# Root mean squares of a two-block transformer: tokens on the partitions of a few columns, then laid out as rows by a product with the identity

## The reference, cut to what matters

```python
def rms_norm(x, g):
    xf = x.astype(jnp.float32)
    y = xf * lax.rsqrt(jnp.mean(xf * xf, axis=-1, keepdims=True) + EPS)
    return (y * g.astype(jnp.float32)).astype(x.dtype)

h = rms_norm(x, norm1_g[l]) * (1.0 + sc1) + sh1      # first block, layers 0 and 1
```

```python
y = rms_norm(y.reshape(bsz, seq, SSM_GROUPS, D_INNER // SSM_GROUPS), ssm_norm_g[l].reshape(SSM_GROUPS, D_INNER // SSM_GROUPS))
```

## Time and profile before

| | us |
|---|---|
| median of 3 runs | 2081.39 (2077.65 to 2081.71) |
| time of the profiled execution | 2083.6 |
| span in the profile | 2081.5 |
| PE busy | 1824.0 (88%) |
| PEld busy | 1730.1 (83%) |
| POOL busy | 1173.7 (56%) |
| DVE busy | 1144.6 (55%) |
| ACT busy | 879.1 (42%) |
| mean granted clock of TensorE | 0.900 |

### The profile page before, as it was taken

How to read it: one execution, slowest core, us unless ns; L and a number is a source line. 1 busy time by engine, 2 the same in 40 slices (tenths; PEclk the granted TensorE clock), 3 DMA queues, 4 the chain that set the end, 5 groups by cost and what they waited for, 6 DMA issues and landing times.

```text
span 2081.5 us, 34069 instructions
## 1 busy us (share of the span) xinstructions
PE 1824.0 (88%) x13514; PEld 1730.1 (83%) x13514; DVE 1144.6 (55%) x1840; ACT 879.1 (42%) x1427; POOL 1173.7 (56%) x480
## 2 busy tenths in 40 slices
PE   8987689999868999679498999967999897967999
PEld 8977689888667999679497888857999796767999
DVE  3289657656633886459946657553685227343410
ACT  2233454544334664224264544333565443334542
POOL 1256665354345899437484445525788676025886
PEclk8689899999979999769799999989999998569999
DMA  6233355343323558334355543524465644013554
GB/s 244 81 111 126 128 173 203 132 162 136 124 91 118 191 189 283 118 102 141 103 168 187 193 132 109 175 80 134 142 185 182 224 154 125 1 40 122 184 186 137
DMA packets 85949, 302.76 MB, mean 145 GB/s; under 512 B 9888, under 2 KB 12960, under 8 KB 85536
## 3 DMA queue, kind: packets, MB, share of 16 engines
q1 hardware_dynamic: 85792, 300.59, 43.8%
HBM read 299.50 MB, written 1.05 MB: 144 GB/s over the span
## 4 chain that ended last, share of the span: by engine, by line
PE 70%; DVE 16%; issue 4%; DVEq 4%; ACT 2%; POOL 2%; DMA 1%; SPq 0%; ACTq 0%; POOLq 0%
PE gemm_bank L1292 53%; PE turn_bank L1400 2%; PE score_bank L1292 2%; POOL w_lo L365 2%; PE outp_bank L1520 1%; PE outp_bank L1385 1%; PE score_bank L1418 1%; PE turn_bank L1367 1%; DVE work L770 1%; DVE work L754 1%; PE score_bank L1367 1%; DVEq L753 1%; PE score_bank L1417 1%; DMA ada_w<-in_w_ada 1%; DVE qkv L781 1%
## 5 line engine op out<-in xcount | busy, mean ns | idle before, releaser
L365 POOL TENSOR_TENSOR w_lo<-w_raw,w_hi 128x1024 fp32r<-128x1024 f32 (+1 forms) x476 | 1173.5, 2473 | 896.2 <-ACT w_hi L383 891.3
L383 ACT ACTIVATE w_hi<-w_raw 128x1024 fp32r<-128x1024 f32 (+1 forms) x476 | 492.6, 1038 | 727.2 <-PE gemm_bank L1292 699.6
L1292 PE MATMUL gemm_bank<-h_hi,w_hi 128*128 128x256 f32 x1984 | 577.7, 291 | 95.4 <-DVE conv L681 32.1
L1292 PE MATMUL gemm_bank<-h_lo,w_hi 128*128 128x256 f32 x1984 | 569.5, 287 | 0.0
L1292 PE MATMUL gemm_bank<-h_hi,w_lo 128*128 128x256 f32 x1984 | 569.2, 287 | 0.0
L1292 PEld LDWEIGHTS gemm_bank<-h_hi,w_hi 128*128 128x128 f32 x1984 | 388.3, 196 | 108.4 <-DVE h_lo L681 33.0
L1292 PEld LDWEIGHTS gemm_bank<-h_lo,w_hi 128*128 128x128 f32 x1984 | 388.2, 196 | 0.1
L1292 PEld LDWEIGHTS gemm_bank<-h_hi,w_lo 128*128 128x128 f32 x1984 | 387.4, 195 | 0.0
L1292 PE MATMUL gemm_bank<-w_hi,h_hi 128*128 128x256 f32 (+3 forms) x736 | 216.9, 295 | 21.5 <-DVE h_lo L681 9.6
L1292 PE MATMUL gemm_bank<-w_lo,h_hi 128*128 128x256 f32 (+3 forms) x736 | 215.8, 293 | 0.0
L1292 PE MATMUL gemm_bank<-w_hi,h_lo 128*128 128x256 f32 (+3 forms) x736 | 215.5, 293 | 0.0
(11 more groups left out here) (256 smaller groups left out, 2814.8 us busy)
## 6 DMA issues: line engine op xcount, KB each, us to landing
w_raw<-in_stream SPq DMA_DIRECT2D x458, 512.0 KB, 3.5
ada_w<-in_w_ada SPq DMA_DIRECT2D x80, 512.0 KB, 4.6
ada_first<-in_w_ada SPq DMA_DIRECT2D x16, 512.0 KB, 11.3
w_raw<-in_stream SPq DMA_DIRECT2D x8, 256.0 KB, 2.6
alibi_sb<-in_alibi SPq DMA_DIRECT2D x1, 1920.0 KB, 8.4
rows_sb<-in_rows SPq DMA_DIRECT2D x1, 1536.0 KB, 11.6
residual<-in_x_t SPq DMA_DIRECT2D x1, 1024.0 KB, 7.2
out_x<-residual SPq DMA_DIRECT2D x4, 256.0 KB, 4.5
```

The costliest lines, as they stand in the source:

```text
L365: nc.gpsimd.tensor_tensor(w_lo[:, s, 0:n], w_raw[:, s, 0:n], w_hi[:, s, 0:n].bitcast(f32), ALU.subtract).then_inc(lo_ready, 1)
L383: A(w_hi[:, s, 0:n], w_raw[:, s, 0:n], ACT.Copy).then_inc(hi_ready, 1)
L1292: ins = M(o, a, b, start=first and i == 0, stop=last and i == len(passes) - 1, skip_group_check=True)
```

## The change

The sum of squares of a token no longer comes as a row repeated on all partitions. The tile of squares becomes the stationary operand, 128 features x 128 tokens, and one column of ones the moving one; the result is one column, with a token on each partition. The 256 tokens give two columns. `square_sum_x` issues 16 such products for 8 before (`column_sum`), and `square_sum` 2 for one. DVE, ACT and again DVE work on 2 columns (an x norm) or 4 (a y norm) in the new tile `rcol`; `root_columns` has the same five operations as `rsqrt`. Then PE lays them out as a row on all partitions: the stationary operand is a column broadcast over 128 columns, the moving one the identity (`row_of_columns`, two products of 128 columns for each row of 256 tokens). The row stays in the PSUM bank, and the scalar_tensor_tensor operations read it from there. The bank is given free behind these, no longer behind the first read of it.

Where the rows are formed: in an x norm right behind the sum (`root_row_x`); for the first norm behind the first of the 8 shift columns; for the first half's y norm in the second half behind chunks 16 to 19 and ahead of the transposes; for the second half's behind chunks 30 and 31. The wait of PE for the constants' arrival stands ahead of the shift columns now.

```diff
             def sum_root(l, which):
-                A(rs[:, 0, :], rs[:, 1, :], ACT.Sqrt).then_inc(x_root, 1)
+                act.wait_ge(x_mean, 2 * l + which + 1)
+                A(rcol[:, 0:TT], rcol[:, 4:4 + TT], ACT.Sqrt).then_inc(x_root, 1)
...
-                    for gi in range(2):
-                        b, k = T.use(l, ts + gi)
-                        act.wait_ge(T.read[b], k + 1)
-                        A(rs[:, gi, :], work[:, gi, 0:SEQ], ACT.Sqrt).then_inc(y_root, 1)
+                    act.wait_ge(y_mean, 2 * l + hf + 1)
+                    A(rcol[:, 0:4], rcol[:, 4:8], ACT.Sqrt).then_inc(y_root, 1)
...
+            def root_columns(n):
+                r, v, w = rcol[:, 0:n], rcol[:, 4:4 + n], rcol[:, 8:8 + n]
+                V.reciprocal(r, r)
+                dve.drain()
+                V.tensor_tensor(w, r, r, ALU.mult)
+                dve.drain()
+                V.tensor_tensor(w, w, v, ALU.mult)
+                dve.drain()
+                V.tensor_scalar(w, w, -0.5, 1.5, ALU.mult, ALU.add)
+                dve.drain()
+                V.tensor_tensor(r, r, w, ALU.mult)
+                return dve.drain()
...
-                dve.wait_ge(o_full, 6 * l + (6 if which else 1))
+                dve.wait_ge(x_sum, n + 1)
+                V.tensor_scalar(rcol[:, 4:4 + TT], O.bank[b][:, 2 * SEQ - TT:2 * SEQ], 1.0 / D, EPS, ALU.mult, ALU.add
+                                ).then_inc(x_mean, 1)
                 if l < DEPTH and which:
                     mods(ada_column(6 * l + 3), KT, O.bank[b][:, SEQ:SEQ + KT])
-                V.tensor_scalar(rs[:, 1, :], O.bank[b][:, 0:SEQ], 1.0 / D, EPS, ALU.mult, ALU.add).then_inc(O.read[b], 1)
                 dve.wait_ge(x_root, n + 1)
-                dve.drain()
-                rsqrt(rs[:, 0, :], rs[:, 1, :], work[:, 0, 0:SEQ])
+                root_columns(TT).then_inc(x_col, 1)
+                dve.wait_ge(o_full, 6 * l + (6 if which else 1))
                 for kt in range(KT):
-                    stt(sq[:, kt, :], XT[:, kt, :], gain[:, kt:kt + 1], rs[:, 0, :], ALU.mult, ALU.mult).then_inc(h_scaled, 1)
+                    stt(sq[:, kt, :], XT[:, kt, :], gain[:, kt:kt + 1], O.bank[b][:, 0:SEQ], ALU.mult, ALU.mult).then_inc(h_scaled, 1)
+                dve.drain().then_inc(O.read[b], 1)
...
-                    dve.wait_ge(y_root, 4 * l + 2 * hf + 2)
-                    dve.drain()
-                    rsqrt(rs[:, 0:2, :], work[:, 0:2, 0:SEQ], work[:, 2:4, 0:SEQ])
+                    ins.then_inc(y_mean, 1)
+                    dve.wait_ge(y_root, 2 * l + hf + 1)
+                    root_columns(4).then_inc(y_col, 1)
                     for f in range(8):
                         t = 8 * hf + f
-                        stt(zg[:, t, :], zg[:, t, :], col("ssmn", t), rs[:, f // 4, :], ALU.mult, ALU.mult).then_inc(y_scaled, 1)
+                        b, k = T.use(l, ts + f // 4)
+                        if f % 4 == 0:
+                            dve.wait_ge(y_row, 4 * l + 2 * hf + f // 4 + 1)
+                        stt(zg[:, t, :], zg[:, t, :], col("ssmn", t), T.bank[b][:, 0:SEQ], ALU.mult, ALU.mult).then_inc(y_scaled, 1)
+                        if f % 4 == 3:
+                            dve.drain().then_inc(T.read[b], 1)
...
-                    ins = M(out[:, 0:SEQ], ones[:, 0:P], sq[:, kt, :], start=kt == 0, stop=kt == KT - 1)
-                ins.then_inc(o_full, 1)
+                    for tt in range(TT):
+                        ins = column_sum(out, tt, sq[:, kt, tt * P:(tt + 1) * P], kt == 0, kt == KT - 1)
+                ins.then_inc(x_sum, 1)
+
+            def column_sum(out, tt, squares, first, last):
+                c = 2 * SEQ - TT + tt
+                return M(out[:, c:c + 1], squares, ones[:, 0:1], start=first and tt == 0, stop=last, skip_group_check=True)
+
+            def row_of_columns(out, c):
+                for tt in range(TT):
+                    ins = M(out[:, tt * P:(tt + 1) * P], rcol[:, c + tt:c + tt + 1].to_broadcast([P, P]), ident[:],
+                            start=True, stop=True)
+                return ins
+
+            def root_row_x(l, which):
+                i = (O_N2 if which else O_N1) if l < DEPTH else (O2_N2 if which else O2_N1)
+                b, k = O.use(l, i)
+                pe.wait_ge(x_col, 2 * l + which + 1)
+                row_of_columns(O.bank[b], 0).then_inc(o_full, 1)
...
             def norm_sum(l, which):
                 square_sum_x(l, which)
+                root_row_x(l, which)
                 return half_h(l, which)
...
+            pe.wait_ge(set_up, 1)
             for a in range(KT):
                 ada_first_column(a)
-            pe.wait_ge(set_up, 1)
+                if a == 0:
+                    root_row_x(0, 0)
...
+                def y_rows(hf):
+                    pe.wait_ge(y_col, 2 * l + hf + 1)
+                    for gi in range(2):
+                        b, k = T.use(l, t_half(hf)[1] + gi)
+                        row_of_columns(T.bank[b], 2 * gi).then_inc(y_row, 1)
...
                     for c in before:
                         scan_chunk(c)
+                    if hf:
+                        y_rows(0)
                     for r in range(4):
...
-                        ins = M(T.bank[b][:, 0:SEQ], ones[:, 0:P], work[:, f % 4, SEQ:2 * SEQ], start=f % 4 == 0, stop=f % 4 == 3)
+                        for tt in range(TT):
+                            ins = column_sum(T.bank[b], tt, work[:, f % 4, SEQ + tt * P:SEQ + (tt + 1) * P], f % 4 == 0, f % 4 == 3)
...
                     for c in after:
                         scan_chunk(c)
+                y_rows(1)
                 pe.wait_ge(y_ready, (l + 1) * 16)
```

More of the change, by code:

```diff
@@ L142, in build @@
         rt = sb("rope_tables", [P, 4, TT, 32])
-        rs = sb("rstd_row", [P, 2, SEQ])
         probs = sb("probs", [P, 2, CW])
@@ L148, in build @@
         small = sb("small", [P, 256])
+        rcol = sb("root_cols", [P, 12])
         root = sb("head_root", [P, 3, 32])
@@ L241, in build @@
             sem("sq_ready"), sem("x_root"), sem("h_scaled"), sem("h_hi_ready"), sem("h_ready"))
+        x_sum, x_mean, x_col = sem("x_sum"), sem("x_mean"), sem("x_col")
+        y_mean, y_col, y_row = sem("y_mean"), sem("y_col"), sem("y_row")
         idx_rot, relu_used = sem("idx_rot"), sem("relu_used")
@@ L408, in sum_root @@
             def sum_root(l, which):
-                i = (O_N2 if which else O_N1) if l < DEPTH else (O2_N2 if which else O2_N1)
-                b, k = O.use(l, i)
-                act.wait_ge(O.read[b], k + 1)
-                A(rs[:, 0, :], rs[:, 1, :], ACT.Sqrt).then_inc(x_root, 1)
+                act.wait_ge(x_mean, 2 * l + which + 1)
+                A(rcol[:, 0:TT], rcol[:, 4:4 + TT], ACT.Sqrt).then_inc(x_root, 1)
             def h_high(l, which, bias):
@@ L1116, in _ @@
                         dve.wait_ge(T.full[b], k + 1)
-                        V.tensor_scalar(work[:, gi, 0:SEQ], T.bank[b][:, 0:SEQ], 1.0 / 512, EPS, ALU.mult, ALU.add
-                                        ).then_inc(T.read[b], 1)
-                    dve.wait_ge(y_root, 4 * l + 2 * hf + 2)
-                    dve.drain()
-                    rsqrt(rs[:, 0:2, :], work[:, 0:2, 0:SEQ], work[:, 2:4, 0:SEQ])
+                        ins = V.tensor_scalar(rcol[:, 4 + 2 * gi:6 + 2 * gi], T.bank[b][:, 2 * SEQ - TT:2 * SEQ], 1.0 / 512, EPS,
+                                              ALU.mult, ALU.add)
+                    ins.then_inc(y_mean, 1)
+                    dve.wait_ge(y_root, 2 * l + hf + 1)
+                    root_columns(4).then_inc(y_col, 1)
                     for f in range(8):
                         t = 8 * hf + f
-                        stt(zg[:, t, :], zg[:, t, :], col("ssmn", t), rs[:, f // 4, :], ALU.mult, ALU.mult).then_inc(y_scaled, 1)
+                        b, k = T.use(l, ts + f // 4)
[4 more added lines that the diff above has]
+                            dve.drain().then_inc(T.read[b], 1)
                     for f in range(8):
```

## The result

The changed kernel takes 2104.57 us (median of 4 runs, 2102.6 to 2108.7) for 2081.55 before (4 runs, 2077.65 to 2082.7); ratio 1.0123, 95% interval 1.0102 to 1.0144. It is slower, as forecast, but by more: the time lies above the range of 2077 to 2101. The profiled execution took 2102.6 us (span 2100.6, mean granted clock 0.900) for 2083.6 (2081.5, 0.900).

A forecast was written before the change was run, and what follows sets the result against it. PE's products were taken to bound the kernel, with stretches where PE waits for DVE. 7.5 - 3.1 - 8.8 + 14.0 = +9.6 us on 2083.6 gives 2093.2, the median put at 2091.0; range for 8 in 10 runs 2077 to 2101.

The forecast's parts named there:

- The start: First x norm: one-column sum brings no clock rise, so sum, shift columns and row cost 7.5 us more on PE.
- the first rival: Sums stay at 2.4 GHz and the start's clock rises as before: -8.8 us, a median of 2072.6; chance 0.12.
- The x norms: Five x norms behind the first: shorter chain gains 9.0 us, one-column sums cost 5.9, a gain of 3.1 us.
- The second halves' norm: Second half's y norm: first scaled tile at 571.6 for 576.02, a gain of 4.4 us a layer, 8.8 together.
- The first halves' norm: First half's y norm: later scaling and slower clock cost 7.0 us a layer, 14.0 both; bounds 0 to 9 a layer.
- 5.8 for PE's order: First half's y norm: the row stands behind chunks 16 to 19 on PE, so DVE scales 5.8 us later.
- 1.2 for the clock: First half's y norm: PE nearly still between 488 and 494, clock likely falls, work behind slower by 0 to 3 us.
- The second rival: The wait behind chunks 16 to 19 is taken up later in the scan: -4.4 us, 2077.0; chance 0.14.
- The third: Rival: column sums in the scan let the clock fall, one in four of 32 y sums, 12 us added: 2103; chance 0.10.

The follow-up runs named there:

- e4: The changed kernel with the first x norm alone done as in the kernel before; 2100.31 us, 1.0088 of the kernel before.
- e2: The changed kernel with the drain behind a y norm's eighth scaling operation moved behind the 8 low-part operations; 2090.82 us, 1.0051 of the kernel before.
- e12: The changed kernel with an ACT copy of 256 columns between the OTH copies and the copy of chunk 20; 2101.57 us, one run.
- e13: e2 with an ACT copy of one column between the OTH copies and the copy of chunk 20; 2107.34 us, one run.
- e9: The kernel before with only the second halves' y norms and the second, fourth and fifth x norms changed; 1.0008 of the kernel before.
- e11: The changed kernel with two unused products of 256 columns behind each of the 16 start columns; 1.0256 of the kernel before.

## Why the prediction was wrong

Its direction held, and three of its four terms came within 2.5 us; the fourth lacked a part, and that part is most of the error.

- The start, +7.5: measured +7.1 in the profiles, 7.3 by e4 with a wide interval. The mechanism is right: the pitch stays at 0.215, which refutes the first rival (the clock does not care). The size is in part luck, since the same kernel before also starts 3 us later in other executions, and the cost is then 4.
- The x norms, -3.1: the chain 2.9 forecast, 2.93 measured. The sums +6.4 for +5.9, but not norm by norm: the two that ran at the half clock before cost 0.3 and 0.8 for the 1.8 and 1.1 forecast, the other three 2.1, 2.0 and 1.2 for 1.0 each. That the total fits is luck. By the whole distance, from the last projection before a norm to the 48th product behind it, the five gain 3.0, a sum that two profiles of the kernel before differ in by 1.1.
- The second halves' norm, -8.8: measured -6.3. The terms left out are POOL's collision with one column operation (0.69), drains (0.4) and the row a little later.
- **The first halves' norm, +14.0 with bounds of 0 and 18: measured +22.6. This is the step that failed.** Its 5.8 for PE's order was 5.86. Its 1.2 for the clock was 0.7 and 1.1. What failed is the sentence that all behind the scaling "moves by the whole 5.8 us": the 8 `OTL` operations were only moved, at their old duration of 2.77. The change puts a drain right ahead of them, and with it there three of them are blocked by POOL's `w_lo`: 6.46 us a layer, 12.9 in two. The prediction had put this term at nothing, without a word on it; the two drains' own 0.4 us a layer were left out too. Against it go the 2.5 and 2.2 us that the scan takes back. e2, which moves the drain and nothing else, measures 1.0051 x 2081.55 = 2092.2 us, so the prediction, 2091.0, had in effect priced that kernel; that they meet within 1.2 us has the luck of the other terms in it.

The Trainium skill (SBUF — State Buffer, section Who interferes with whom) says that a DVE operation with two SBUF inputs and a GpSimd operation that reads SBUF exclude each other. The trace agrees: 2.56 us for a low part of 0.42. The `OTL` operation and `w_lo` both have this form, and they stand side by side in the profile of before (above), where the cost fell on POOL and did not show; the rule does not say who wins in a series, which in e2, e12 and e13 goes with the drain.

- The sum: 7.1 - 3.0 - 6.3 + 22.6 = +20.4 in the profiles, whose own difference is 19.1. The other 1.3 was not traced; an unchanged stretch such as the start can differ by 3 us between two executions of one kernel. The medians differ by 23.0, and the interval of the ratio is 21 to 30, so up to some 5 us (25.6 by the ratio) stand in no term; the first profile of before lay 2 us above its median, the one after 2 us below.
- The second rival (the wait is taken up later) holds for 2.5 and 2.2 us a layer. The third (column sums let the clock fall in the scan) has the counts for it, behind the last sum of a second half alone: 14 of 28 such norms in 14 kernels, 1.5 to 2.7 us each. Behind the other y sums it was not counted. It was not in the changed kernel's profile, and so is not shown to be a part of its loss; at half of two norms it would add some 2 us to its median (my estimate from these counts). In e9's profile it takes 5 of the 11 us by which e9 missed. The rest of e9 stays open; its late start explains nothing, since this start, which e9 leaves as it was, is late in six of ten profiles.

## What to carry to other kernels

When a change moves a series of operations or puts a drain ahead of it, ask again which engine shares a port with it at the new place, and price the series blocked (one operation of the other engine each) as well as free. A reduction with a thin result has fewer columns but here twice the instructions (32 for 16), each with its weight load, and part of its price stands in the clock of the work behind it. A wait that is cheap on the waiting engine can be long by the order of the engine that releases it: look up where that engine's instruction stands.

## What was not expected of the hardware

- With a drain ahead of a series of two-input DVE operations POOL blocked 2 to 4 of the 8, 2.6 us each for 0.42, at arrivals of 1.26 to 1.65 us; without it none at 1.56 and 1.65, and POOL's operation took 3.3 to 3.4 us for some 2.4.
- PE, without a gap, stayed at 1.2 GHz for 62 us (6.43 to 68.85) in which all but four of its instructions had one column, and two wide products, 2.05 us in each 5.1, didn't change it (e11). The granted clock of the profile reads 1.00 from 6 to 26 us, though the pitch of 0.215 there is that of the half clock: in the first stretch only the pitch tells.
- Executions differ in how long the half clock lasts, also of one kernel: 386 to 451 us at a granted clock of 0.50 in the profiles of these kernels, 416 and 399 in the two of the kernel before.
